# Score matmuls over 66 partitions, four convolution taps on TensorE, and three moved pieces of weight splitting in a two-block transformer kernel

## The chip, the cores and the metric

The kernel runs on one core of one Trainium2 chip. The metric is device time in microseconds; lower is better. The engines are named as in the profile: PE is TensorE, DVE is VectorE, ACT is ScalarE, POOL is GpSimd and SP is SyncE, which issues the loads.

## The reference

256 tokens of width 1024 pass through three layers. The first has an attention of 8 heads of 64 beside a causal depthwise convolution of 31 taps over 512 channels, then a gated feed-forward of width 2816. The second is a forgetting attention ("fox") of 16 heads of 64 with another such feed-forward; the third is a state-space mixer (S5) with a third feed-forward. Cut to what the change touches:

```python
q = apply_rope(rms_norm(q, q_norm_g[l]), cos, sin)      # first attention, per head of 64
k = apply_rope(rms_norm(k, k_norm_g[l]), cos, sin)
s_own = jnp.einsum('bhqd,bhkd->bhqk', qc, k_own).astype(jnp.float32) * scale
...
h = lax.conv_general_dilated(h, dw_w[:, None, :], ..., feature_group_count=CONV_WIDTH)   # 31 taps
x = x + jnp.concatenate([attn, conv], axis=-1) @ w_out[l]
x = x + (jax.nn.silu(h @ w_gate[l]) * (h @ w_up[l])) @ w_down[l]
...
log_f = jax.nn.log_sigmoid(f_logit + b_f)               # fox: one forget logit per head and token
c = jnp.cumsum(log_f, axis=1).transpose(0, 2, 1)
s = s + c[:, :, q0:k_end, None] - c[:, :, None, :k_end]
```

## The kernel before

All weights are read once, in units of 128 x 2048 float32 values (1 MB). SP loads a unit into one of four slots of `wraw`. ACT writes its high part (`split_high`, line 416) into a ring of two slots `whi`, and DVE the rest, the low part (`split_low`, line 422), into `wlo`. TensorE multiplies high and low parts of weights and of activations in three fp32r matmuls (lines 462 to 464, 482 to 484, 510) that add up in PSUM. Some units have other places for their parts (`early_gain`, `early_nat`, `early_qt`, with the low part over `wraw`). Each engine's order is written out by hand in `build`, and semaphores tie them together; an engine never passes an instruction that waits. A "quarter" (`mm_quarter`) is a quarter of a unit's contraction, six matmuls for both rows of 128 tokens.

*Ahead of the first attention* the units are q (0, 1), k (2, 3), u of the convolution (4 to 7) and v (8, 9). TensorE turns two heads at a time (`pe_heads`, line 1148) into two PSUM banks in alternation, and does one quarter of v after each such group; ACT copies the groups into `qt1` and `kt1` (`act_heads`, line 1188). ACT takes four sigmoids of u (`csig`, line 2020), and DVE multiplies them in (`glu`).

*In the first attention* each head has its scores (`scores`, lines 1055 and 1056: a 128x128 and a 128x256 matmul, each followed by a bf16 matmul that adds the mask), the maximum on DVE (line 1124), the exponential on ACT (line 1105), a turn on TensorE (line 1065) and the values (line 1074). Between them stand taps of the convolution: channel group 3 whole (31 taps, line 1631) and the last 10 taps of group 2 (line 1640) run on TensorE as matmuls with diagonal matrices that ACT makes (`tap_diagonals`, `shared_diagonals`); DVE does the other taps (line 2363). A float32 matmul is recorded as two.

*Into the feed-forward and into the fox units* (`add_and_turn` on DVE, `act_row_turn` on ACT, `mm_first_rows` on TensorE) the residual is added row by row of 128 tokens, turned on TensorE in tiles, and each turned tile is split into `actH` by ACT (line 630) and `actL` by DVE (line 637), while TensorE already multiplies the first two units with the tiles that are there.

*The forget gate* runs among the first fox units: `forget_logits` within the second unit, a copy `fT` on DVE, `forget_turned` on TensorE (two small transposes, line 1697), then on DVE and ACT the log of a sigmoid (lines 2509 to 2516, 2102, 2104), and its sums on TensorE (lines 1710 to 1712) ahead of the fifth fox unit. DVE's low part of the fourth fox unit stands within that arithmetic.

Of the kernel before, what the change touches and what calls it, by code (L numbers as in the profile page):

```python
# [17 lines left out]
F32 = mybir.dt.float32  # L18
# [3 lines left out]
ALU = mybir.AluOpType  # L22
AX = mybir.AxisListType

P = 128
TOK = 256
RT = TOK // P
D = 1024
KT = D // P
# [4 lines left out]
HD = 64  # L34
H1 = 8
H2 = 16
AW = H1 * HD
TAPS = 31
TAPG = 8
SHARED = 10  # L40
TAIL_PAIRS = {21: 19, 23: 20}
DIAGONALS_AT = {2: (0,), 3: (1, 2), 4: (3,), 5: (4,)}
U_BANKS = (2, 3, 6, 7)
ROWS_LOW, ROWS_HIGH = (0, 1, 2, 3), (4, 5, 6, 7)
# [9 lines left out]
UNIT = 2048  # L54
# [10 lines left out]
class Program:  # L65
# [121 lines left out]
    def place(self):  # L187
# [91 lines left out]
        self.csig = pen("csig", [P, 4, TOK])  # L279
        self.qn, self.kn = pen("qn", [P, RT, AW]), pen("kn", [P, RT, AW])  # L280
        self.vn = pen("vn", [P, RT, AW])
        self.qt, self.kt1 = pen("qt1", [HD, H1, TOK]), pen("kt1", [HD, H1, TOK])
        self.p1 = pen("p1", [P, 2, 384])
# [20 lines left out]
        pen = Pen(R0)  # L304
        AUG = HD + 2
        self.qa, self.ka = pen("qa", [P, RT, H2, AUG]), pen("ka", [P, RT, H2, AUG])
# [111 lines left out]
    def split_low(self, dve, n0, it=0):  # L418
# [4 lines left out]
                          self.high_of(n0).bitcast(F32), ALU.subtract).then_inc(self.lo_done, 1)  # L423

    def load_first(self, sp, view):

        for k in range(4):
            done = self.landed[0] if k == 3 else self.sem(f"first_landed{k}")
            sp.dma_start(self.wraw[:, 0, 512 * k:512 * k + 512], view[:, k, :]).then_inc(done, 16)
# [57 lines left out]

    def mm_first_rows(self, pe, st, n0, banks, order, between):


        for r, h in order:
            pe.wait_ge(self.lo_done, n0 + h + 1)
            for k in range(4):
                if (r, h, k) in between:
                    between[(r, h, k)]()
                pe.wait_ge(*self.past(st + "_act_ready", self.turn_count(st, r, 4 * h + k) + 1))
                self.mm_quarter(pe, n0 + h, banks, h, k, low=(self.lo_done, n0 + h + 1), rows=(r,))

# [419 lines left out]
    def pe_ffn(self, pe, st, turn, prep=False, last_units=1, half=None, end=None):  # L918
        n = self.first[st + ".up"]
        if st == "f1":  # L920
            self.mm_first_rows(pe, st, n, self.pair_banks(0), UNIT_BY_UNIT,
                               {(0, 0, 2): lambda: turn(1, 0), (0, 1, 2): lambda: turn(1, 1)})
# [289 lines left out]
def pool_constants(m, pool):  # L1212

    c = Chain(pool, m.sem("pool_chain"))
    for t, v in ((m.ident, 0.0), (m.ones, 1.0), (m.tri, 1.0), (m.swap, 0.0), (m.zerob, 0.0), (m.identb, 0.0), (m.maskb, 0.0),
                 (m.mhalf, -0.5), (m.halfpi, math.pi / 2), (m.hpad[:, :, 0:TAPS - 1], 0.0)):
        c.step(pool.memset(t[:] if not isinstance(t, bass.AP) else t, v))
# [224 lines left out]
def build(nc, io, out):  # L1442
    with ExitStack() as ctx:
# [145 lines left out]
        def _(pe):  # L1589
# [21 lines left out]
            m.pe_heads(pe, "a1", m.qn[:].rearrange("p r (h d) -> p r h d", d=HD), (0, H1), "q_ready", 2, (4, 5), 0,  # L1611
                       v_quarter)
            m.pe_heads(pe, "a1", m.kn[:].rearrange("p r (h d) -> p r h d", d=HD), (0, H1), "k_ready", 2, (4, 5),
                       H1 // 2, lambda f: v_quarter(4 + f))
# [3 lines left out]
            def conv(i):  # L1618

                if i == 3:  # L1620
                    pe.wait_ge(*m.past("v_out", 2))
                pair = i if i < 19 else TAIL_PAIRS.get(i)
                if pair is None:
# [70 lines left out]
            def forget_turned():  # L1694
                pe.wait_ge(*m.past("f_out", 1))
                for r in range(RT):
# [5 lines left out]
                            {(0, 0, 2): lambda: fp_turn(1, 0), (0, 1, 2): lambda: fp_turn(1, 1),  # L1702
                             (1, 1, 2): forget_logits})
            m.mm_half_k(pe, n + 2, (4, 5), 0)
            forget_turned()
            m.mm_half_k(pe, n + 3, (4, 5), 1)
# [242 lines left out]
        def _(act):  # L1949
# [67 lines left out]
            act.wait_ge(*m.past("k_head_sums", 1))  # L2017
            for j in range(4):
                act.wait_ge(m.used, first["u"] + 3 + j // 2)
                act.activation(m.csig[:, j, :], ps[:, U_BANKS[2 + j // 2], (j % 2) * TOK:(j % 2 + 1) * TOK],  # L2020
                               ACT.Sigmoid, bias=m.vec[:, GLUB + 4 + j:GLUB + 5 + j]).then_inc(sem("sig"), 1)
            act.activation(rinv[:, 0, 0:1], m.halfpi[:], ACT.Exp)
            m.act_heads(act, "a1", m.qt, (0, 4), (4, 5), 0)
            m.split_high(act, 9)
            m.act_heads(act, "a1", m.qt, (4, H1), (4, 5), 2)
            m.split_high(act, 10)
# [66 lines left out]
            m.act_row_turn(act, "fp", ROWS_HIGH, 1, range(4), MIXPRE)  # L2093
            for r in range(RT):
                m.act_row_turn(act, "fp", ROWS_HIGH, r, range(4, KT), MIXPRE)
            forget_high()
            m.split_high(act, first["fox"] + 2)
            for r in range(RT):
# [223 lines left out]
        def _(dve):  # L2322
# [55 lines left out]
            def head_norm1(st, banks, t, ki, rows):  # L2378
# [4 lines left out]
                for r in rows:  # L2383
                    rs = (m.rs, m.rsk)[ki][:, 8 * r:8 * r + 8].unsqueeze(2).to_broadcast([P, 8, HD])
                    c(dve.tensor_tensor(hd(m.rtmp[:]), hd(ps[:, banks[r], :]), rs, ALU.mult))
                    tb = [m.ropeg[:, ki, r, i:i + 1, :].to_broadcast([P, 8, HD]) for i in range(2)]
                    c.step(dve.tensor_tensor(hd(t[:, r, :]), hd(m.rtmp[:]), tb[0], ALU.mult))
                    halves = m.rtmp[:].rearrange("p (h a d) -> p h a d", a=2, d=32)
# [4 lines left out]
                    c.wait()  # L2393
                    dve.tensor_tensor(t[:, r, :], t[:, r, :], m.rtmp2[:], ALU.add).then_inc(sem(st + "_ready"), 1)
                    dve.wait_ge(*m.past(st + "_ready", r + 1))
# [16 lines left out]
            for j in range(2):  # L2412
                glu(j)
            conv(8)
            for j in range(2, 4):
# [67 lines left out]
            def add_and_turn(st, base, out, used, banks, gain, second_unit):  # L2483
# [3 lines left out]
                m.dve_row_turn(dve, st, banks, 1, range(4), gain)  # L2487
                m.split_low(dve, second_unit)
                m.dve_row_turn(dve, st, banks, 0, range(4, KT), gain)
                m.dve_row_turn(dve, st, banks, 1, range(4, KT), gain)  # L2490
# [11 lines left out]
            dve.wait_ge(*m.past("f_done", 1))  # L2502
            dve.tensor_copy(m.fT[:], ps[0:H2, 3, 0:TOK]).then_inc(sem("f_out"), 1)

            dve.wait_ge(*m.past("f_turned", 1))
            dve.wait_ge(*m.past("fb_in", 16))
            dve.wait_ge(*m.past("fp_rstd", RT))
            for r in range(RT):
# [4 lines left out]
               .then_inc(sem("f_abs"), 1)  # L2513
            m.split_low(dve, n + 3)
            dve.wait_ge(*m.past("f_ln", 1))
# [278 lines left out]
```

## Time and profile before

| | us |
|---|---|
| median of 3 runs (lowest, highest) | 989.36 (989.02, 989.72) |
| profiled execution | 988.04 |
| its span, first to last instruction | 986.2 |
| PE busy | 963.3 (98%) |
| DVE busy | 583.5 (59%) |
| ACT busy | 506.9 (51%) |
| POOL busy | 310.8 (32%) |

Times in the trace run from the start of the span. Busy times of matmuls overlap, since they are pipelined, so what a group of matmuls costs is read from start to start. A row of a timeline gives start, duration, engine, source line, operation, output and inputs, shape and count; the brackets give the idle time of the engine ahead of it and what ended it.

### The profile page before, as it was taken

The page shows a single profiled execution, that of the slowest core. Times are in us where ns is not written, and L with a number is a line of the kernel's source. Part 1 is how long each engine was busy: PE and PEld are TensorE (multiplying, and loading weights), DVE is VectorE, ACT ScalarE, POOL GpSimd, SP SyncE. Part 2 cuts the span into 40 slices and gives each one's busy share as a digit, 9 for nine tenths or more (in the row PEclk, how much of TensorE's full clock was granted, in tenths as well). Part 3 has the DMA queues.
Part 4 walks back from the last instruction along what each step waited for, and adds up shares of the span by engine and source line. Part 5 has one row for each costly group of instructions (what it writes and reads, how often), then busy time and mean ns, then how long its engine had stood idle before and what let it go on. Part 6 is the DMA issues. An engine that isn't in the chain of part 4 may idle for free.

```text
span 986.2 us, 14283 instructions
## 1 busy us (share of the span) xinstructions
PE 963.3 (98%) x5446; PEld 800.2 (81%) x5446; DVE 583.5 (59%) x639; ACT 506.9 (51%) x723; POOL 310.8 (32%) x331
## 2 busy tenths in 40 slices
PE   8999999999999989999999999999989999999997
PEld 6977777888888868888888888888978888888886
DVE  4898875554554456565774545546586755545544
ACT  6855465444443467456654444434456564444332
POOL 5670447999699216763010000000000020000000
PEclk9999999999999999999999999999999999999999
DMA  9842026676776746545446657557946456557551
GB/s 335 271 136 86 1 90 220 224 224 222 264 230 225 223 147 212 162 164 171 129 147 199 187 173 241 185 206 247 381 167 215 128 173 197 185 172 254 172 170 43
DMA packets 133827, 186.79 MB, mean 189 GB/s; under 512 B 5904, under 2 KB 104720, under 8 KB 133264
## 3 DMA queue, kind: packets, MB, share of 16 engines
q1 hardware_dynamic: 109632, 158.28, 49.3%
q10 hardware_dynamic: 24144, 27.81, 8.2%
q8 instruction: 35, 0.57, 0.3%
q14 instruction: 16, 0.13, 0.0%
HBM read 174.54 MB, written 15.73 MB: 193 GB/s over the span
## 4 chain that ended last, share of the span: by engine, by line
PE 91%; DVE 5%; ACT 2%; issue 1%; POOL 0%; DVEq 0%; POOLq 0%; ACTq 0%
PE ps L510 25%; PE ps L482 16%; PE ps L484 16%; PE ps L483 16%; PE ps L1055 2%; PE ps L462 2%; PE ps L464 2%; PE ps L463 2%; PE ps L839 1%; PE ps L1631 1%; PE ps L1074 1%; DVE wlo L422 1%; PE ps L1065 1%; PE ps L621 1%; PE ps L1160 1%
## 5 line engine op out<-in xcount | busy, mean ns | idle before, releaser
L422 DVE TENSOR_TENSOR wlo<-wraw,whi 128x2048 fp32r<-128x2048 f32 x127 | 302.0, 2380 | 293.1 <-ACT whi L416 293.1
L416 ACT ACTIVATE whi<-wraw 128x2048 fp32r<-128x2048 f32 x127 | 243.2, 1915 | 255.4 <-PE ps L484 156.3
L482 PE MATMUL ps<-whi,actH 128*128 128x512 f32 x640 | 258.0, 403 | 6.8 <-DVE wlo L422 5.9
L484 PE MATMUL ps<-whi,actL 128*128 128x512 f32 x640 | 250.2, 391 | 0.0
L483 PE MATMUL ps<-wlo,actH 128*128 128x512 f32 x640 | 249.4, 390 | 0.0
L482 PEld LDWEIGHTS ps<-whi,actH 128*128 128x128 f32 x640 | 120.3, 188 | 33.7 <-DVE wlo L422 6.5
L484 PEld LDWEIGHTS ps<-whi,actL 128*128 128x128 f32 x640 | 120.1, 188 | 26.1
L756 POOL TENSOR_SCALAR ss<-ss 128x1 f32<-128x1 f32 x8 | 1.8, 221 | 436.1 <-ACT sg L726 436.1
L483 PEld LDWEIGHTS ps<-wlo,actH 128*128 128x128 f32 x640 | 120.5, 188 | 22.3
L510 PE MATMUL ps<-whi,gH 128*128 128x512 f32 x248 | 77.8, 393 | 0.0
L510 PE MATMUL ps<-wlo,gH 128*128 128x512 f32 x248 | 76.8, 390 | 0.0
L510 PE MATMUL ps<-whi,gL 128*128 128x512 f32 x248 | 76.8, 389 | 0.0
L510 PEld LDWEIGHTS ps<-whi,gL 128*128 128x128 f32 x248 | 46.6, 188 | 9.8
L510 PEld LDWEIGHTS ps<-wlo,gH 128*128 128x128 f32 x248 | 46.6, 188 | 9.8
L510 PEld LDWEIGHTS ps<-whi,gH 128*128 128x128 f32 x248 | 45.9, 188 | 10.2 <-issue 1.2
L462 PE MATMUL ps<-actH,whi 128*128 128x256 f32 x160 | 45.6, 285 | 0.2 <-DVE wlo L422 0.2
L463 PE MATMUL ps<-actL,whi 128*128 128x256 f32 x160 | 45.3, 283 | 0.0
L464 PE MATMUL ps<-actH,wlo 128*128 128x256 f32 x160 | 45.3, 283 | 0.0
L877 ACT ACTIVATE gH<-ps 128x512 f32 (+1 forms) x33 | 19.8, 599 | 42.0 <-PE ps L839 42.0
L1105 ACT ACTIVATE p<-ps,nmax 128x128 f32<-128x128 f32 (+1 forms) x48 | 19.7, 417 | 34.6 <-DVE nmax L1124 34.6
L2363 DVE SCALAR_TENSOR_TENSOR cacc<-hpad,vectors,cacc 128x256 f32<-128x256 f32 x80 | 36.0, 521 | 0.0
L983 POOL TENSOR_TENSOR otmp<-G,Bri 128x512 f32 (+1 forms) x16 | 31.3, 1958 | 0.0
(452 smaller groups left out, 1573.7 us busy)
## 6 DMA issues: line engine op xcount, KB each, us to landing
wraw<-in_ffn_w_gate SPq DMA_DIRECT2D x44, 512.0 KB, 4.0
wraw<-in_ffn_w_up SPq DMA_DIRECT2D x44, 512.0 KB, 4.9
wraw<-in_ffn_w_down SPq DMA_DIRECT2D x18, 1024.0 KB, 4.9
wraw<-in_fox_w_in SPq DMA_DIRECT2D x16, 1024.0 KB, 5.4
wraw<-in_w_gate SPq DMA_DIRECT2D x22, 512.0 KB, 4.1
wraw<-in_w_up SPq DMA_DIRECT2D x22, 512.0 KB, 5.0
wraw<-in_w_in SPq DMA_DIRECT2D x9, 1024.0 KB, 11.2
wraw<-in_w_down SPq DMA_DIRECT2D x9, 1024.0 KB, 5.0
```

The lines of the kernel that those rows point to most:

```text
L416: act.activation(self.high_of(n0), self.wraw[:, n0 % RAW, :], ACT.Copy).then_inc(self.hi_done, 1)
L422: dve.tensor_tensor(self.low_of(n0), self.wraw[:, n0 % RAW, :], self.high_of(n0).bitcast(F32), ALU.subtract).then_inc(self.lo_done, 1)
L462: pe.matmul(out, wh, self.actH[:, k, :], start=(i == 0), stop=False)
L463: pe.matmul(out, wh, self.actL[:, k, :], start=False, stop=False)
L464: last = pe.matmul(out, wl, self.actH[:, k, :], start=False, stop=(i == KT - 1))
L482: pe.matmul(out, xh, wh, start=(ka == 0), stop=False)
L483: pe.matmul(out, xh, wl, start=False, stop=False)
L484: last = pe.matmul(out, xl, wh, start=False, stop=(ka == KT - 1))
L510: last = pe.matmul(self.ps[:, base + 2 * r + c, :], x, w[c], start=st, stop=sp_)
L877: act.activation(self.g_tiles(self.gH, f, f_step), self.ps[:, self.turn_bank(f0, at_end), :].rearrange("p (a b) -> p a b", a=2), ACT.Copy)\
L983: return pool.tensor_tensor(out, f[:, g, :].unsqueeze(3).to_broadcast([P, GB, n, SC]), w[:, g, :].unsqueeze(2).to_broadcast([P, GB, n, SC] ...
L2363: i = dve.scalar_tensor_tensor(m.cacc[:, j, :], src, w, m.cacc[:, j, :], ALU.mult, ALU.add)
```

## The change

1. `qn` and `kn` get two more columns a head, filled with zeros by POOL at the start, so that turned heads and scores have 66 partitions in place of 64.
2. `SHARED` goes from 10 to 14: four more taps of group 2 on TensorE, four fewer on DVE, whose taps are dealt out anew over the heads; the slots on TensorE and the diagonals on ACT follow.
3. Unit 9's high part goes between the sigmoids on ACT, its low part ahead of the last two `glu` on DVE.
4. In the first feed-forward and the fox units, the second unit's low part is made in two halves with two turned tiles between them, and the third unit's high part goes among ACT's turned tiles.
5. `forget_turned` goes into the third fox unit, and the fourth unit's low part ahead of the forget gate's arithmetic on DVE.

```diff
-SHARED = 10
-TAIL_PAIRS = {21: 19, 23: 20}
-DIAGONALS_AT = {2: (0,), 3: (1, 2), 4: (3,), 5: (4,)}
+SHARED = 14
+TAIL_PAIRS = {23: 22}
+DIAGONALS_AT = {3: (0, 1), 4: (2, 3), 5: (4, 5), 6: (6,)}
+AUG = HD + 2
...
-        self.qn, self.kn = pen("qn", [P, RT, AW]), pen("kn", [P, RT, AW])
+        self.qn, self.kn = pen("qn", [P, RT, H1, AUG]), pen("kn", [P, RT, H1, AUG])
...
-        self.qt, self.kt1 = pen("qt1", [HD, H1, TOK]), pen("kt1", [HD, H1, TOK])
+        self.qt, self.kt1 = pen("qt1", [AUG, H1, TOK]), pen("kt1", [AUG, H1, TOK])
...
+    def low_half(self, dve, n, i):
+
+        cols = slice(i * UNIT // 2, (i + 1) * UNIT // 2)
+        dve.wait_ge(self.hi_done, n + 1)
+        dve.tensor_tensor(self.low_of(n)[:, cols], self.wraw[:, n % RAW, cols],
+                          self.high_of(n)[:, cols].bitcast(F32), ALU.subtract)\
+           .then_inc(self.lo_done if i == 1 else self.sem("half_low"), 1)
...
         for r, h in order:
-            pe.wait_ge(self.lo_done, n0 + h + 1)
             for k in range(4):
...
-                self.mm_quarter(pe, n0 + h, banks, h, k, low=(self.lo_done, n0 + h + 1), rows=(r,))
+                first_half = half_low is not None and (r, h) == (0, 1) and k < 2
+                low = self.past("half_low", half_low) if first_half else (self.lo_done, n0 + h + 1)
+                self.mm_quarter(pe, n0 + h, banks, h, k, low=low, rows=(r,))
...
-                 (m.mhalf, -0.5), (m.halfpi, math.pi / 2), (m.hpad[:, :, 0:TAPS - 1], 0.0)):
+                 (m.mhalf, -0.5), (m.halfpi, math.pi / 2), (m.hpad[:, :, 0:TAPS - 1], 0.0),
+                 (m.qn[:, :, :, HD:AUG], 0.0), (m.kn[:, :, :, HD:AUG], 0.0)):
...
-                pair = i if i < 19 else TAIL_PAIRS.get(i)
+                pair = i if i < 22 else TAIL_PAIRS.get(i)
...
-            m.mm_half_k(pe, n + 2, (4, 5), 0)
-            forget_turned()
+            for k in range(4):
+                m.mm_quarter(pe, n + 2, (4, 5), 0, k)
+                if k == 1:
+                    forget_turned()
...
             for j in range(4):
+                if j == 2:
+                    m.split_high(act, 9)
                 act.wait_ge(m.used, first["u"] + 3 + j // 2)
...
-            m.act_heads(act, "a1", m.qt, (0, 4), (4, 5), 0)
-            m.split_high(act, 9)
-            m.act_heads(act, "a1", m.qt, (4, H1), (4, 5), 2)
+            m.act_heads(act, "a1", m.qt, (0, H1), (4, 5), 0)
...
-            for r in range(RT):
-                m.act_row_turn(act, "f1", ROWS_LOW, r, range(4, KT), N2)
+            m.act_row_turn(act, "f1", ROWS_LOW, 0, (4, 5), N2)
             m.split_high(act, 16)
+            m.act_row_turn(act, "f1", ROWS_LOW, 0, (6, 7), N2)
+            m.act_row_turn(act, "f1", ROWS_LOW, 1, range(4, KT), N2)
...
-            conv(4)
-            m.split_low(dve, 9)
-            conv(6)
+            conv(11)
             m.split_low(dve, 10)
...
-                    conv((6, 10, 11, 11, 11, 11, 2, 3)[h])
+                    conv((7, 8, 6, 9, 9, 9, 8, 4)[h])
```

Left out here: the low part of unit 9 goes behind `conv(8)` on DVE, and the fox units get on ACT what the last ACT piece gives unit 16. On DVE, around the fox units, the order was this (`wrawlow` is the second unit's low part, the first `wlo` the third unit's, the second the fourth's, `fl` the forget gate):

```order
L637 SCALAR_TENSOR_TENSOR actL<-ps,vectors,actH 128x128 x4
L422 TENSOR_TENSOR wrawlow<-wraw,early_nat 128x2048
L637 SCALAR_TENSOR_TENSOR actL<-ps,vectors,actH 128x128 x8
L2500 TENSOR_TENSOR wfL<-wf,wfH 128x128
L422 TENSOR_TENSOR wlo<-wraw,whi 128x2048
L2503 COPY fT<-ps 16x256
L2509 SCALAR_TENSOR_TENSOR fl<-ps,rx,fb 128x16 x2
L2512 SCALAR_TENSOR_TENSOR fl<-fl 128x32
L422 TENSOR_TENSOR wlo<-wraw,whi 128x2048
L2516 SCALAR_TENSOR_TENSOR fl<-fl 128x32
```

With the change it is this on the same engine, at the same place:

```order
L646 SCALAR_TENSOR_TENSOR actL<-ps,vectors,actH 128x128 x4
L429 TENSOR_TENSOR wrawlow<-wraw,early_nat 128x1024
L646 SCALAR_TENSOR_TENSOR actL<-ps,vectors,actH 128x128 x2
L429 TENSOR_TENSOR wrawlow<-wraw,early_nat 128x1024
L646 SCALAR_TENSOR_TENSOR actL<-ps,vectors,actH 128x128 x6
L2516 TENSOR_TENSOR wfL<-wf,wfH 128x128
L422 TENSOR_TENSOR wlo<-wraw,whi 128x2048
L2519 COPY fT<-ps 16x256
L422 TENSOR_TENSOR wlo<-wraw,whi 128x2048
L2526 SCALAR_TENSOR_TENSOR fl<-ps,rx,fb 128x16 x2
L2529 SCALAR_TENSOR_TENSOR fl<-fl 128x32
L2532 SCALAR_TENSOR_TENSOR fl<-fl 128x32
```

The second unit's low part is split around two tiles, and the fourth unit's low part has moved ahead of the three `fl` steps, the first of which waits for TensorE's turn.

On ACT, ahead of the first attention, the order was this (`csig` are the sigmoids, the first `whi` here is unit 9's high part, the second unit 10's):

```order
L2020 ACT_TABLE_LOAD
L2020 ACTIVATE csig<-ps,vectors 128x256 x4
L2022 ACT_TABLE_LOAD
L2022 ACTIVATE rinv<-halfpi 128x1
L1188 ACTIVATE qt_128<-ps 64x512 x2
L416 ACTIVATE whi<-wraw 128x2048
L1188 ACTIVATE qt_128<-ps 64x512 x2
L416 ACTIVATE whi<-wraw 128x2048
L1188 ACTIVATE kt_129<-ps 64x512 x4
```

With the change:

```order
L2034 ACT_TABLE_LOAD
L2034 ACTIVATE csig<-ps,vectors 128x256 x2
L416 ACTIVATE whi<-wraw 128x2048
L2034 ACTIVATE csig<-ps,vectors 128x256 x2
L2036 ACT_TABLE_LOAD
L2036 ACTIVATE rinv<-halfpi 128x1
L1197 ACTIVATE qt_128<-ps 66x512 x4
L416 ACTIVATE whi<-wraw 128x2048
L1197 ACTIVATE kt_129<-ps 66x512 x4
```

Unit 9's high part has moved ahead of two sigmoids and of all copies of queries.

## Rows read from the trace of the kernel before

**Rows 1.** The list of cores: span and mean granted clock.
```profile
core 0: 986.2 us, clock 0.999
```

**Rows 2.** The page's chain that ended last, shares of the span by engine.
```profile
PE 91%; DVE 5%; ACT 2%; issue 1%; POOL 0%; DVEq 0%; POOLq 0%; ACTq 0%
```

**Rows 3.** PE's waits, the two longest: us in total, times, longest us.
```profile
PE ps L482 <- DVE wlo L422: 5.9, 3, 2.9
PE ps L569 <- POOL zero L1234: 3.9, 1, 3.9
```

**Rows 4.** Timeline of PE ahead of the first attention: third and fifth head group, unit 9.
```profile
60.78 0.60 PE L1148 MATMUL ps<-ident,qn 128*64 128x128 f32 x4
...
64.44 0.60 PE L1148 MATMUL ps<-ident,kn 128*64 128x128 f32 x4
67.24 0.50 PE L482 MATMUL ps<-whi,actH 128*128 128x512 f32 x1 [2.21 <-DVE wlo L422]
```

**Rows 5.** Timeline of DVE there: first taps and unit 9's low part.
```profile
57.44 3.56 DVE L2363 SCALAR_TENSOR_TENSOR cacc<-hpad,vectors,cacc 128x256 f32<-128x256 f32 x6
...
64.36 2.83 DVE L422 TENSOR_TENSOR wlo<-wraw,whi 128x2048 fp32r<-128x2048 f32 x1
```

**Rows 6.** Timeline of ACT there: the last two sigmoids, the first two query copies.
```profile
57.33 0.84 ACT L2020 ACTIVATE csig<-ps,vectors 128x256 f32<-128x256 f32 x2 [1.63 <-PE ps L464]
...
59.59 1.06 ACT L1188 ACTIVATE qt<-ps 64x512 f32<-64x512 f32 x2
```

**Rows 7.** Timeline of PE in the first attention, one head: taps, scores, taps, turn, next scores.
```profile
86.70 1.08 PE L1631 MATMUL ps<-hpad,dtaps 128*128 128x256 f32 x4
87.71 0.48 PE L1055 MATMUL ps<-kt,qt 64*128 64x128 f32 x2
...
88.98 1.08 PE L1631 MATMUL ps<-hpad,dtaps 128*128 128x256 f32 x4
89.90 0.49 PE L1065 MATMUL ps<-ident,p 128*128 128x128 f32 x3
...
92.72 0.49 PE L1055 MATMUL ps<-kt,qt 64*128 64x128 f32 x2
```

**Rows 8.** Timeline of PE in the second attention: first score matmul, what follows the scores.
```profile
389.43 0.39 PE L1055 MATMUL ps<-kt,qt 66*128 66x128 f32 x2
...
390.23 0.48 PE L482 MATMUL ps<-whi,actH 128*128 128x512 f32 x1
```

**Rows 9.** Timeline of DVE in the first attention: the taps of one head.
```profile
91.94 4.44 DVE L2363 SCALAR_TENSOR_TENSOR cacc<-hpad,vectors,cacc 128x256 f32<-128x256 f32 x11
```

**Rows 10.** Timelines of PE and DVE, first feed-forward: second and third unit, second unit's low part.
```profile
146.43 0.47 PE L482 MATMUL ps<-early_nat,actH 128*128 128x512 f32 x1 [0.47 <-DVE actL L637]
154.19 0.50 PE L482 MATMUL ps<-whi,actH 128*128 128x512 f32 x1 [0.77 <-DVE wlo L422]
143.64 2.43 DVE L422 TENSOR_TENSOR wrawlow<-wraw,early_nat 128x2048 fp32r<-128x2048 f32 x1
```

**Rows 11.** Timelines of PE, ACT and DVE in the fox units: second, fourth and fifth unit.
```profile
351.17 0.47 PE L482 MATMUL ps<-early_nat,actH 128*128 128x512 f32 x1 [0.34 <-DVE actL L637]
365.56 0.29 PE L1697 MATMUL ps<-ident,fT 16*128 16x16 f32 x2
368.75 0.50 PE L482 MATMUL ps<-whi,actH 128*128 128x512 f32 x1 [2.90 <-DVE wlo L422]
374.90 0.48 PE L482 MATMUL ps<-whi,actH 128*128 128x512 f32 x1
358.93 1.90 ACT L416 ACTIVATE whi<-wraw 128x2048 fp32r<-128x2048 f32 x1
372.33 2.29 DVE L422 TENSOR_TENSOR wlo<-wraw,whi 128x2048 fp32r<-128x2048 f32 x1 [0.58 <-ACT whi L416]
```

**Rows 12.** Timeline of POOL at the start: the fill of hpad.
```profile
1.87 0.20 POOL L1217 MEMSET hpad<- 128x120 f32 x1
```

More of the change, by code:

```diff
@@ L304, in place @@
         pen = Pen(R0)
-        AUG = HD + 2
         self.qa, self.ka = pen("qa", [P, RT, H2, AUG]), pen("ka", [P, RT, H2, AUG])
@@ L486, in mm_quarter, with mm_first_rows @@
             last.then_inc(self.used, 1)
-    def mm_first_rows(self, pe, st, n0, banks, order, between):
+    def mm_first_rows(self, pe, st, n0, banks, order, between, half_low=None):
         for r, h in order:
-            pe.wait_ge(self.lo_done, n0 + h + 1)
             for k in range(4):
@@ L921, in pe_ffn @@
             self.mm_first_rows(pe, st, n, self.pair_banks(0), UNIT_BY_UNIT,
-                               {(0, 0, 2): lambda: turn(1, 0), (0, 1, 2): lambda: turn(1, 1)})
+                               {(0, 0, 2): lambda: turn(1, 0), (0, 1, 2): lambda: turn(1, 1)}, 1)
         else:
@@ L1610, in _ @@
             pe.wait_ge(*m.past("k_ready", 2))
-            m.pe_heads(pe, "a1", m.qn[:].rearrange("p r (h d) -> p r h d", d=HD), (0, H1), "q_ready", 2, (4, 5), 0,
+            m.pe_heads(pe, "a1", m.qn, (0, H1), "q_ready", 2, (4, 5), 0,
                        v_quarter)
-            m.pe_heads(pe, "a1", m.kn[:].rearrange("p r (h d) -> p r h d", d=HD), (0, H1), "k_ready", 2, (4, 5),
+            m.pe_heads(pe, "a1", m.kn, (0, H1), "k_ready", 2, (4, 5),
                        H1 // 2, lambda f: v_quarter(4 + f))
@@ L1702, in _ @@
                             {(0, 0, 2): lambda: fp_turn(1, 0), (0, 1, 2): lambda: fp_turn(1, 1),
-                             (1, 1, 2): forget_logits})
-            m.mm_half_k(pe, n + 2, (4, 5), 0)
-            forget_turned()
+                             (1, 1, 2): forget_logits}, 2)
+            for k in range(4):
+                m.mm_quarter(pe, n + 2, (4, 5), 0, k)
+                if k == 1:
+                    forget_turned()
             m.mm_half_k(pe, n + 3, (4, 5), 1)
@@ L2093, in _ @@
             m.act_row_turn(act, "fp", ROWS_HIGH, 1, range(4), MIXPRE)
-            for r in range(RT):
-                m.act_row_turn(act, "fp", ROWS_HIGH, r, range(4, KT), MIXPRE)
+            m.act_row_turn(act, "fp", ROWS_HIGH, 0, (4, 5), MIXPRE)
+            m.split_high(act, first["fox"] + 2)
+            m.act_row_turn(act, "fp", ROWS_HIGH, 0, (6, 7), MIXPRE)
+            m.act_row_turn(act, "fp", ROWS_HIGH, 1, range(4, KT), MIXPRE)
             forget_high()
-            m.split_high(act, first["fox"] + 2)
             for r in range(RT):
@@ L2386, in head_norm1 @@
                     tb = [m.ropeg[:, ki, r, i:i + 1, :].to_broadcast([P, 8, HD]) for i in range(2)]
-                    c.step(dve.tensor_tensor(hd(t[:, r, :]), hd(m.rtmp[:]), tb[0], ALU.mult))
+                    heads = t[:, r, :, 0:HD]
+                    c.step(dve.tensor_tensor(heads, hd(m.rtmp[:]), tb[0], ALU.mult))
                     halves = m.rtmp[:].rearrange("p (h a d) -> p h a d", a=2, d=32)
@@ L2393, in head_norm1 @@
                     c.wait()
-                    dve.tensor_tensor(t[:, r, :], t[:, r, :], m.rtmp2[:], ALU.add).then_inc(sem(st + "_ready"), 1)
+                    dve.tensor_tensor(heads, heads, hd(m.rtmp2[:]), ALU.add).then_inc(sem(st + "_ready"), 1)
                     dve.wait_ge(*m.past(st + "_ready", r + 1))
@@ L2414, in _ @@
             conv(8)
+            m.split_low(dve, 9)
             for j in range(2, 4):
                 glu(j)
-            conv(4)
-            m.split_low(dve, 9)
-            conv(6)
+            conv(11)
             m.split_low(dve, 10)
@@ L2487, in add_and_turn @@
                 m.dve_row_turn(dve, st, banks, 1, range(4), gain)
-                m.split_low(dve, second_unit)
-                m.dve_row_turn(dve, st, banks, 0, range(4, KT), gain)
+                m.low_half(dve, second_unit, 0)
+                m.dve_row_turn(dve, st, banks, 0, (4, 5), gain)
+                m.low_half(dve, second_unit, 1)
+                m.dve_row_turn(dve, st, banks, 0, (6, 7), gain)
                 m.dve_row_turn(dve, st, banks, 1, range(4, KT), gain)
@@ L2503, in _ @@
             dve.tensor_copy(m.fT[:], ps[0:H2, 3, 0:TOK]).then_inc(sem("f_out"), 1)
+            m.split_low(dve, n + 3)
             dve.wait_ge(*m.past("f_turned", 1))
@@ L2513, in _ @@
                .then_inc(sem("f_abs"), 1)
-            m.split_low(dve, n + 3)
             dve.wait_ge(*m.past("f_ln", 1))
```

## The prediction

> **What bounds the kernel now.** I read the list of cores first: the span is 986.2 us at a granted clock of 0.999, so TensorE stays at its upper level and no idle stretch in the span has lowered it [rows 1]. The chain of work that ended last is next: PE (TensorE) holds 91% of it, DVE (VectorE) 5%, ACT (ScalarE) 2% [rows 2]. So a change counts if it shortens TensorE's own work or one of the few stretches in which TensorE waits. The list of TensorE's waits gives the largest of those: the low part of a weight unit that DVE has not finished, 5.9 us in three places, and the start, where TensorE waits 3.9 us for GpSimd's constants [rows 3]. The rest is timelines of the places that the change edits. The sum is made against the profiled execution (988.04 us), which lies 1.32 us below the median of the runs shown (989.36); I apply the sum to the median.
>
> **1. Unit 9 earlier, before the first attention.** TensorE turns the heads of q and k in eight groups and does one quarter of the value units behind each. The fifth group starts at 64.44, and the quarter behind it, the first one of unit 9, only at 67.24, after 2.21 us of idle time that DVE's low part ends [rows 4]. That low part ran from 64.36 to 67.19, behind taps of the convolution [rows 5]. In the change the high part of unit 9 stands on ACT ahead of the third and fourth sigmoid, and the low part on DVE behind the first eight taps. Those sigmoids started at 57.33, when TensorE had finished the last u unit [rows 6]; the high part's ring slot comes free with the same unit, so it starts at 57.33 too and takes 1.90 (the same 128x2048 copy in [rows 11]). DVE's first taps end at 57.44 + 3.56 = 61.0, the low part (2.83) at 63.8, before TensorE wants it: the 2.21 us go. Late next are the query copies: behind the moved copy the first of them slips on ACT from 59.59 to 61.45 [rows 6]; half of the 1.06 for a pair later, at 62.0, its bank is free. TensorE's third group, at 60.78 [rows 4], needs that bank and now waits 1.2. After that the copies run in a row and find TensorE busy. So 2.2 − 1.2 = **1.0 us gained**; bounds 2.2 (no new wait) and 0.
>
> **2. Scores over 66 rows, four taps moved.** In the first attention the score matmuls of a head contract over 64 partitions: from the first (87.71) to the tap that follows (88.98) they take 1.27 us [rows 7]. In the second attention, where heads already have 66 partitions, the same four matmuls, of the same 128 and 256 columns, take 0.80 us (389.43 to 390.23) [rows 8]. That is 0.47 a head, 3.8 for eight. Two taps ahead of the scores take 1.01 (86.70 to 87.71), two behind them 0.92 (88.98 to 89.90) [rows 7]; if the 0.09 is the way into the other form, it goes too: 4.5. I take 4.2. Four more taps on TensorE at 0.46 each (half of 0.92) cost 1.8. Net **2.4 us gained**, bounds 2.0 and 2.7, as long as TensorE sets the pace. DVE does as much: eleven taps took 4.44 us, 0.40 each [rows 9], and the two reductions fill the rest of a head's 5.01 (87.71 to 92.72 [rows 7]), 0.6. With the change DVE has nine taps a head at most, 4.2 us, and TensorE 5.01 − 0.5 = 4.5. Both shrink, which either edit alone would not give: fewer rows' time on TensorE alone leaves DVE at 5.0. The diagonals of the extra taps go onto ACT, two pairs a head, where ACT waits for the reductions; I cost them at nothing, and if that cover is gone the tap behind them waits.
>
> **3. Halves in the first feed-forward.** TensorE idles 0.47 us before the second unit of the first pair (146.43) and 0.77 us before the third unit (154.19) [rows 10]. The first wait: DVE did the whole low part (2.43 us from 143.64 [rows 10]) and then the turned tiles that TensorE wanted. In the change it does half of it ahead of them, so they come 1.2 earlier, and 0.47 is less than that. The other half is due only two quarters and a turn of tiles later. The second wait: the third unit's high part stood on ACT behind all turned tiles and now stands ahead of the last six, so that DVE can take its low part as soon as its own turns end. Gain 0.47 + 0.77 = **1.2 us**; bounds 0.5 (only the first) and 1.3.
>
> **4. The fox units.** The same halves remove the 0.34 us at 351.17. The large wait is the 2.90 us at 368.75, for the low part of the fourth fox unit [rows 11]. Its high part was done at 360.8 (358.93 + 1.90), but on DVE the low part stood behind the forget gate's arithmetic, which needs a turn that TensorE did at 365.56, after the whole third unit. In the change the low part stands ahead of that arithmetic, and the turn comes after two quarters of the third unit. The low part can end at 360.8 + 2.3 = 363.1, TensorE asks for it at 365.85: the wait goes. The turn itself only changes place. Late next is the fifth unit: its low part ran from 372.33 to 374.62 and TensorE took it at 374.90, 0.28 later [rows 11]. TensorE comes 3.2 earlier; ACT's way to that unit (exponential, logarithm, key block, squares, high part) begins with the turn, which comes about 3 earlier as well. So 0.1 may remain: **3.1 us gained**, bounds 1.5 (the way to unit five moves by half) and 3.3.
>
> **5. Start.** GpSimd has two more small fills ahead of the constants on which TensorE starts; the fill of hpad, with more elements, took 0.20 [rows 12]. I take 0.2 for both, bounds 0 and 0.4. The copies of heads and the writes of qn and kn have as many columns as before: nothing.
>
> **Sum:** −1.0 − 2.4 − 1.2 − 3.1 + 0.2 = −7.5 us; 989.36 − 7.5 = **981.9 us** (980.5 against the profiled execution). Behind these places TensorE has no other wait of this size [rows 3], and the loads are released by its units and DVE's low parts, so what is gained is kept.
>
> [...] By rows 7 and 8, 64 rows cost 0.47 us a head more than 66. [...]
>
> **Rivals.**
> *66 rows gain nothing.* If the 0.47 belongs to the neighbours (taps in one attention, weight units in the other) and not to the 64 rows, part 2 is only its cost: −7.5 + 4.2 = −3.3, 986.1 us. For it: the neighbours do differ. Against it: between 87.71 and 88.98 there is no neighbour, and the whole difference is there. [...] Chance 0.06.
> *The time comes back at the next unit.* In part 4 the fifth unit and in part 1 the query copies are late next. If parts 4 and 1 gain only their lower bounds (1.5 and 0), the sum is −4.9: 984.5 us. For it: the slack at the fifth unit is 0.28. Against it: the work ahead of it starts with the turn that is moved. Chance 0.12.
> *Slower: the clock.* The new wait of 1.2 us near 60.8 lies just ahead of the first attention. If the granted clock fell there to its lower level (half) and stayed so through the heads, their 8 x 4.5 = 36 us on TensorE would take up to 36 more. From 7.5 us of work at the lower level on, the kernel is slower than before; with 12 it is at 993.9. Against it: waits of 2.21 and 2.90 us are in this span, whose clock is 0.999. Chance 0.02.
>
> **How the numbers follow.** A measurement of this kernel can tell 0.2%, 2 us, from no change. My forecast has 0.78, the two weaker gains 0.12 and 0.06, the clock 0.02; 0.02 is left for the two weaker gains at once, which lands near 989. Faster by over 2 us: 0.96, less 0.01 for the first rival with a weak part 3: 0.95. Slower 0.02, same 0.03. All upper bounds at once (2.2, 2.7, 1.3, 3.3, no cost) would be −9.5, 979.9 us, the low end. The high end takes in the second rival and reaches 985.2 for one more part at its lower bound.
>
> **What would show it.** Right: no idle time of TensorE before the fourth fox unit and the third feed-forward unit; some 1.2 us of it before the third head group and none before unit 9; score groups of 0.80 us; heads of some 4.5 us. Wrong: score groups still of 1.27; over 1 us of wait at the fifth fox unit; TensorE waiting for diagonals of taps or for DVE's reductions in the attention; a granted clock below 0.99.

## The result, and the profile after

| | before | with the change |
|---|---|---|
| median of 5 runs (lowest, highest) | 989.36 (989.02, 991.63) | 979.54 (979.15, 980.41) |
| profiled execution / its span | 988.04 / 986.2 | 980.41 / 978.5 |

The ratio is 0.9898, 95% interval 0.9884 to 0.9913: 9.8 us faster. The forecast was 7.5 us and 981.9; the measured time lies 0.36 below the low end, 979.9. But the two profiled executions differ by 7.63 only. So a reader who has just the two traces sees almost exactly the forecast, and 2.2 us of the gain are in neither. Where they are is the main question of what follows.

First the chain that ended last and TensorE's two longest waits, after (us in total, times, longest us):

```profile
PE 94%; DVE 3%; ACT 2%; issue 1%; POOL 0%; DVEq 0%; POOLq 0%; ACTq 0%
```
```profile
PE ps L578 <- POOL zero L1244: 4.1, 1, 4.1
PE ps L1157 <- ACT qt L1197: 1.1, 1, 1.1
```

PE's share of the chain went from 91 to 94%. The 5.9 us of waits for a low part in [rows 3] are gone; the second line is the new wait that the prediction expected at the third head group. PE in the v stage, in one head, and around the forget turn (start, duration, engine, line, operation, output and inputs, shape; idle time ahead in brackets):

```profile
62.87 0.63 PE L1157 MATMUL ps<-ident,qn 128*66 128x128 f32 x4 [1.12 <-ACT qt L1197]
...
85.58 0.38 PE L1064 MATMUL ps<-kt,qt 66*128 66x128 f32 x2
85.81 0.22 PE L1065 MATMUL ps<-maskb,identb 128*128 128x128 bf16 x1
85.86 0.65 PE L1064 MATMUL ps<-kt,qt 66*128 66x256 f32 x2
86.35 0.22 PE L1065 MATMUL ps<-maskb,identb 128*128 128x128 bf16 x1
86.41 1.08 PE L1641 MATMUL ps<-hpad,dtaps 128*128 128x256 f32 x4
...
90.06 0.38 PE L1064 MATMUL ps<-kt,qt 66*128 66x128 f32 x2
...
142.86 0.39 PE L490 MATMUL ps<-early_nat,actH 128*128 128x512 f32 x1
...
149.96 0.50 PE L490 MATMUL ps<-whi,actH 128*128 128x512 f32 x1
...
358.03 0.29 PE L1707 MATMUL ps<-ident,fT 16*128 16x16 f32 x2
...
361.11 0.39 PE L490 MATMUL ps<-whi,actH 128*128 128x512 f32 x1
...
367.15 0.50 PE L490 MATMUL ps<-whi,actH 128*128 128x512 f32 x1
```

The score group takes 0.83 us (85.58 to 86.41) where [rows 7] have 1.27, and a head 4.48 in place of 5.01. No bracket stands before the second and third unit of the feed-forward (142.86, 149.96), where [rows 10] have 0.47 and 0.77, nor before the fourth fox unit (361.11), where [rows 11] have 2.90, nor before the fifth (367.15), which the prediction named as late next.

The timeline of PE, cut at five landmarks, gives a table by stage for every trace of this study: *start* is the time of the first head group, *v* from there to the first score of the first attention, *a1* to the channel sums behind it, *o1* from the next turn to the second unit of the first feed-forward, *f1, fox* from there to the first score of the second attention. From that score to the end of TensorE's last matmul it takes 590.7 to 591.0 us in all traces; this is left out, as is the stretch between a1 and o1 (1.92 or 1.93, but in one run).

| trace | start | v | a1 | o1 | f1, fox |
|---|---|---|---|---|---|
| before, 988.04 | 57.12 | 17.23 | 37.54 | 32.62 | 243.00 |
| with the change, 980.41 | 57.92 | 15.91 | 35.10 | 32.00 | 238.85 |
| difference | +0.80 | −1.32 | −2.44 | −0.62 | −4.15 |

Behind the start that is 8.5 us; the start takes back 0.8, of which the fills explain 0.11 (first matmul at 4.06 in place of 3.95). The rest is TensorE's pace. TensorE's 24 turns of the input begin at 7.33 before and at 7.45 with the change; the rows are the same microsecond of both (length, busy time and number of these turns, clock, DMA share, GB/s), first before, then with the change:

```profile
9.00:10.00 1.00, 1.00 (x11) 1.00 1.02 393
9.00:10.00 1.00, 1.00 (x6) 1.00 1.06 403
```

Early turns start 0.21 us apart and later ones 0.11. The pace changes where the trace's own records of the granted clock begin, 8.56 us before and 10.06 with the change; ahead of the first record the column shows 1.00 all the same. So until then TensorE turns at half its later pace (0.21 against 0.11), and 1.50 us more of that are 0.75 of the 0.8. In the sixteen traces of this study the records begin between 5.07 and 10.06.

### The profile page after: what moved, and what is told of

It is laid out like the page before. It is cut to its first block, busy times and chain, and to the rows that moved or that the text cites. A ratio compares the mean times of both kernels' runs of the same rounds, so it can differ in the third digit from the quotient of the medians.

```text
span 978.5 us, 14303 instructions
## 1 busy us (share of the span) xinstructions
PE 961.0 (98%) x5454; PEld 803.0 (82%) x5454; DVE 581.8 (59%) x637; ACT 507.0 (52%) x727; POOL 309.9 (32%) x333
## 4 chain that ended last, share of the span: by engine, by line
PE 94%; DVE 3%; ACT 2%; issue 1%; POOL 0%; DVEq 0%; POOLq 0%; ACTq 0%
PE ps L519 25%; PE ps L490 17%; PE ps L492 16%; PE ps L491 16%; PE ps L470 2%; PE ps L1064 2%; PE ps L472 2%; PE ps L471 2%; PE ps L848 1%; PE ps L1641 1%; PE ps L1083 1%; PE ps L1074 1%; PE ps L630 1%; PE ps L1169 1%; PE ps L1020 1%
## 5 line engine op out<-in xcount | busy, mean ns | idle before, releaser
L1010 POOL TENSOR_TENSOR ob<-ob,otmp 128x576 f32<-128x576 f32 x16 | 34.6, 2160 | 1.3
```

The costliest lines, as they stand in the source:

```text
L1010: pool.tensor_tensor(o, o, t[:], ALU.add).then_inc(done, 1)
```

## The experiments

**The kernel before, three traces more.** The change's runs lie closer together than those of before, so the first question was whether the first trace of before is a typical one.

> The kernel before, unchanged, to get a second trace of it. Its first profiled span (986.2 us, 988.04 us in all) lies 1.3 us below the median of its runs, and the change's (978.5, 980.41) 0.9 us above the median of its own; so the two traces differ by 7.7 us and the medians by 9.8. Theory A: the difference lies in the start, where the 24 turns of the input took 3.56 us (7.33 to 10.89) before and 4.21 us (7.45 to 11.66) with the change, with the granted clock at 1.00 in both, and where the pace of the turns doubles near 8.7 before and near 10.0 with the change. Then this trace has a span of 987 to 988.5, the heads' turns begin at 58 or later instead of 57.12, and from there to the first score of the second attention it takes the same 332.3 us within 0.3. Rival B: the excess over 986.2 lies behind the start, in waits that the first trace lacks: start within 0.3 of 57.12, and over 1 us more behind it.

The median was 989.32. Its 11 runs and 40 more of before beside the other experiments lie in three clusters: 14 at 987.8 to 988.5, 27 at 988.9 to 989.9, 10 at 991.3 to 992.2. The first trace is of the lowest. This one, 991.71, is of the highest, and both theories fell short. The start was longer, 57.72, but v took 18.81 and f1, fox 244.6: 1.6 us more each, behind waits of the same length. The granted clock shows why. The rows are stretches of 2 us: length, PE busy (matmuls), clock, DMA share, GB/s:

```profile
368.00:370.00 2.00, 0.00 (x0) 1.00 0.79 295
370.00:372.00 2.00, 1.12 (x4) 0.91 0.97 227
372.00:374.00 2.00, 2.00 (x6) 0.50 1.00 394
374.00:376.00 2.00, 2.00 (x8) 0.73 1.01 382
```

TensorE idles 2.90 us for the low part of the fourth fox unit, and behind that the clock falls to 0.50: 6 matmuls in 2 us. Behind the 2.25 us for unit 9 it did the same, with 5 matmuls from 68 to 70 us. In the first trace the clock stayed up behind the same wait of 2.90, with 10 matmuls in 2 us:

```profile
368.00:370.00 2.00, 1.25 (x5) 1.00 0.93 231
370.00:372.00 2.00, 2.00 (x10) 1.00 1.01 396
```

Are the runs around the median between the two?

> The kernel before again, for a third trace. The runs of it so far lie in three clusters, near 988.0, near 989.3 and near 991.6 us; the trace at 988.04 has no fall of the granted clock, the one at 991.71 has two, behind the wait for unit 9 and behind the wait for the fourth fox unit. Theory: a run near 989.3 has one, behind the fourth fox unit, with 1.6 us more than the first trace from there to the first score of the second attention, and the rest of the difference in the start. Rival: the fall of such a run is in the v stage.

> The kernel before once more, for a fourth trace, with the same expectations as the run beside it: two falls of the granted clock near 991.6 us, one behind the fourth fox unit near 989.3, none near 988.0.

989.43 and 989.33: each has one fall, and not at the same place, so that theory and rival each held once. The first trace below (989.43) falls in the fox units, v is 17.23 and f1, fox 244.55; the second (989.33) falls in the v stage, 18.82 and 242.96.

```profile
368.00:370.00 2.00, 1.49 (x6) 1.00 0.99 289
370.00:372.00 2.00, 2.00 (x6) 0.50 1.00 367
372.00:374.00 2.00, 2.00 (x7) 0.65 0.93 336
```
```profile
66.00:68.00 2.00, 0.98 (x4) 1.00 0.00 0
68.00:70.00 2.00, 2.00 (x9) 0.58 0.83 287
70.00:72.00 2.00, 2.00 (x7) 0.56 0.58 238
```

So in these traces the clusters are none, one or two falls of the clock at 1.55 to 1.6 us, behind the two waits that the change removes. The runs without a trace agree in their mean granted clock: 0.999 or 1.000 in every run of the lowest cluster, 0.996 to 0.998 in the middle one, 0.993 to 0.996 in the highest. The start of these two was 56.95 and 56.87.

**The fox order back.**

```diff
             for k in range(4):
                 m.mm_quarter(pe, n + 2, (4, 5), 0, k)
-                if k == 1:
-                    forget_turned()
+            forget_turned()
...
-            m.split_low(dve, n + 3)
```
(on DVE the low part goes back in front of the last `fl` instruction)

> The change with the forget turn again behind the whole third fox unit, and the fourth unit's low part again within the forget gate's arithmetic; the halves are kept. My theory: TensorE waits 2.7 to 3.0 us again for the low part of the fourth fox unit, and none of it is taken back later: 982.2 to 982.7 us. Rival (the wait moves on to the fifth unit anyway): under 1.5 us more than with the change, under 981.0.

984.19, 4.65 more than the change, above the expectation: f1, fox took 243.42, 4.57 more. 2.90 is the wait, in the trace as it was; the rest is a fall of the clock to 0.50 behind it, and all five runs lie within 984.14 to 984.33.

**The same wait, filled.**

```diff
             forget_turned()
+            m.keep_warm(pe, 7, 12)
             m.mm_half_k(pe, n + 3, (4, 5), 1)
```

> The kernel with the forget gate's order of before (the run before it at 984.2), with 12 bf16 matmuls on 512 columns into a bank that nobody reads, put on TensorE ahead of the fourth fox unit, where it waits 2.9 us for the low part. Theory A (the fall of the granted clock behind that wait comes from TensorE's idling): the wait still costs its 3.0 us, but the clock stays at 1.00 behind it and the 1.6 us go: 982.4 to 982.9. Rival B (the fall has nothing to do with the idle time): 984.2 or more, with a stretch at 0.5.

983.17 (982.08 to 983.26): theory A by the trace. The wait keeps its price, f1, fox is 241.79, 2.94 more than with the change; the clock stays up and 1.63 us of the run before are gone. The median is 0.3 above the expectation; the runs spread by 1.2, and the three at 983.2 were not traced. Their mean granted clock, 0.999, is above the 0.998 of the traced run, whose clock falls only behind TensorE's last matmul (0.72 from 976 to 978 us, 0.50 from 978 to 980); so no fall shows in them either. First the run with the wait idle, then with it filled:

```profile
360.00:362.00 2.00, 0.26 (x3) 1.00 0.89 335
362.00:364.00 2.00, 0.85 (x2) 0.84 0.90 214
364.00:366.00 2.00, 2.00 (x6) 0.50 0.93 358
```
```profile
360.00:362.00 2.00, 2.00 (x11) 1.00 0.82 305
362.00:364.00 2.00, 1.80 (x9) 1.00 0.96 226
```

So it is TensorE's idling that lets the clock fall there: to 0.50 behind 2.90 us of it, and not with the 0.20 us of it that the filling leaves.

**Unit 9 back.**

```diff
-                if j == 2:
-                    m.split_high(act, 9)
...
+            m.act_heads(act, "a1", m.qt, (0, 4), (4, 5), 0)
+            m.split_high(act, 9)
+            m.act_heads(act, "a1", m.qt, (4, H1), (4, 5), 2)
```
(and the low part again behind `conv(4)`, which follows the last `glu`)

> The change with unit 9's two parts where they were (high part between the query copies, low part behind the second taps). TensorE should wait 2.2 us for that low part again and lose the 1.1 us wait at the third head group: +1.1 us on the way from the heads' turns to the first score. Theory A (a wait of over 2 us lets the granted clock fall to 0.5 behind it in part of the executions, at 1.6 us a fall): the runs lie in two clusters, near 980.6 and near 982.2, with a fall in the v stage in those of the upper one. Rival B (the fall comes from something else, or only where two waits of this size are in the span): all runs near 980.6.

980.53 (980.26 to 981.34): rival B. The wait is there again (2.23 at 67.79), v is 17.15, 1.24 more than with the change, but the mean clocks of the five runs are 0.999 to 1.000, where runs of before with one fall have 0.996 to 0.998. A wait of this length was followed by a fall in two of four traces of before (2.25 and 2.24 us; not behind 2.21 in the two others); in these five runs none shows. What decides it is open.

**64 rows.**

```diff
+ROWS1 = HD
...
-        self.qn, self.kn = pen("qn", [P, RT, H1, AUG]), pen("kn", [P, RT, H1, AUG])
+        self.qn, self.kn = pen("qn", [P, RT, H1, ROWS1]), pen("kn", [P, RT, H1, ROWS1])
```
(the same for `qt` and `kt1`, and without the two fills)

> The change with 64 rows in place of 66 in the first attention, all else kept (fourteen shared taps too). My theory: 64 rows cost 0.47 us a head, so a score group goes from 0.83 back to 1.27 to 1.30 us, and from the first score to the channel sums it takes 35.1 + 3.5 to 4.0 = 38.6 to 39.1 us; the time is 983.0 to 983.6. Rival (the neighbours, not the rows, set the score group): 0.83 a group and 35.1 us, 979.5 in all.

983.74; a1 took 39.31, 0.53 a head more than with 66 rows. Both lie just above what was expected, by 0.1 and 0.2. PE, one head:

```profile
86.42 0.48 PE L1065 MATMUL ps<-kt,qt 64*128 64x128 f32 x2
86.84 0.23 PE L1066 MATMUL ps<-maskb,identb 128*128 128x128 bf16 x1
87.00 0.70 PE L1065 MATMUL ps<-kt,qt 64*128 64x256 f32 x2
87.63 0.23 PE L1066 MATMUL ps<-maskb,identb 128*128 128x128 bf16 x1
87.69 1.08 PE L1641 MATMUL ps<-hpad,dtaps 128*128 128x256 f32 x4
```

From a score to its mask matmul it takes 0.42 and 0.63 here, 0.23 and 0.49 with 66 rows; from the first mask to the next score 0.16 and 0.05. The taps ahead of the first score take 1.01 in place of 0.92. The loss stands at each passage between 64 and 128 rows. To tell it from a slower matmul, the passages were halved:

```diff
+            for i, mask in enumerate((self.maskb, self.zerob, self.maskb)):
+                pe.matmul(self.ps[:, b, i * P:(i + 1) * P], self.identb[:], mask[:], start=(i == 0), stop=False)
             for r in range(RT):
...
-                out = self.ps[:, b, c0:c0 + nk]
-                pe.matmul(out, qt[:, h, r * P:(r + 1) * P], kt[:, h, 0:nk], start=True, stop=False)
-                last = pe.matmul(self.ps[:, b, c0 + nk - P:c0 + nk], self.identb[:], self.maskb[:],
-                                 start=False, stop=True)
+                last = pe.matmul(self.ps[:, b, c0:c0 + nk], qt[:, h, r * P:(r + 1) * P], kt[:, h, 0:nk],
+                                 start=False, stop=(r == 1))
```

> The change with 64 rows, as in the run with 64 rows, but with a head's mask matmuls (and one of zeros, so that all columns are opened) put ahead of its two score matmuls instead of each behind one: TensorE goes from 128 rows to 64 and back once a head, not twice. Only the stretch of the first attention is read. Theory A (the passage between 64 and 128 rows costs): half of the 0.53 us a head goes, less 0.06 for the matmul of zeros: a head takes 4.75 to 4.85 us (5.01 with 64 rows, 4.47 with 66), the stretch from the first score to the channel sums 37.4 to 38.0 us. Rival B (a matmul of 64 rows is slower in itself, or its weight load): 5.0 us a head or more, 39.3 us or more.

```profile
86.04 0.22 PE L1063 MATMUL ps<-maskb,identb 128*128 128x128 bf16 x1
86.09 0.22 PE L1063 MATMUL ps<-zerob,identb 128*128 128x128 bf16 x1
86.15 0.22 PE L1063 MATMUL ps<-maskb,identb 128*128 128x128 bf16 x1
86.30 0.92 PE L1066 MATMUL ps<-kt,qt 64*128 64x128 f32 x4
87.14 1.13 PE L1641 MATMUL ps<-hpad,dtaps 128*128 128x256 f32 x4
...
90.84 0.22 PE L1063 MATMUL ps<-maskb,identb 128*128 128x128 bf16 x1
```

A head takes 4.80 us (86.04 to 90.84), a1 37.50: theory A. Less the 0.05 of the matmul of zeros, one way into 64 rows and back costs 0.27 a head (4.75 against 4.48), two cost 0.53, so nothing is left for the rows themselves. This run also passes between bf16 and float32 only once a head; that costs nothing visible, since with 66 rows a score follows its mask matmul after 0.05 (85.81 to 85.86), as here one mask matmul follows another (86.04 to 86.09).

**Ten shared taps.**

```diff
-SHARED = 14
+SHARED = 10
...
-                    conv((7, 8, 6, 9, 9, 9, 8, 4)[h])
+                    conv((6, 10, 10, 11, 11, 11, 2, 3)[h])
```
(`TAIL_PAIRS`, `DIAGONALS_AT` and the number of taps ahead of the tail as before)

> The change with 10 shared taps on TensorE and 83 on VectorE as before, 66 rows kept. My theory: VectorE then sets the pace, eleven taps and two reductions of a head need 5.0 us, so TensorE's 1.3 us shorter head buys little and the stretch from the first score to the channel sums takes 36.5 to 37.5 us in place of 35.1: 981 to 982 us. Rival (TensorE alone sets the pace): four taps of 0.45 less, 33.3 us, 977.7 us.

982.64, a1 37.02. VectorE sets the pace: TensorE waits 1.92 us for the last heads' exponentials, which follow VectorE's maxima. The clock falls behind this wait too:

```profile
104.86 0.55 PE L1074 MATMUL ps<-ident,p 128*128 128x128 f32 x3 [1.92 <-ACT p L1114]
```
```profile
108.00:110.00 2.00, 2.00 (x12) 0.50 0.00 0
110.00:112.00 2.00, 2.00 (x6) 0.50 0.00 0
112.00:114.00 2.00, 2.00 (x9) 0.62 0.00 0
```

At 0.50 the clock stays for 6.8 us here, and for 3.4 in each of the five other falls ahead of TensorE's last matmul. The same turn and value matmuls as with the change take 1.30 us more at the end of a1, and from a1 to o1 it takes 3.52 in place of 1.92; so it cost 2.9. Without it a1 would be 35.7, worked out from these rows: below the 36.5 to 37.5 that were expected, well above the rival's 33.3. So the mechanism held, and the stretch reached the expected size only by the fall; the time is 0.6 above the expectation. One of the five runs, 980.55 at a clock of 0.998 (the others 0.996), lies 2 us below the others.

**The halves back**, in both places:

```diff
-                m.low_half(dve, second_unit, 0)
-                m.dve_row_turn(dve, st, banks, 0, (4, 5), gain)
-                m.low_half(dve, second_unit, 1)
-                m.dve_row_turn(dve, st, banks, 0, (6, 7), gain)
+                m.split_low(dve, second_unit)
+                m.dve_row_turn(dve, st, banks, 0, range(4, KT), gain)
```
(and the third unit's high part on ACT behind all turned tiles)

> The change with the second unit's low part made at once again and the third unit's high part behind all turned tiles, in the first feed-forward and in the fox units. My theory: the waits 0.47, 0.77 and 0.34 us come back, 1.4 to 1.6 us, all too short for the clock: 980.9 to 981.2, granted clock as with the change. Rival (these waits are taken back at the next unit): under 0.7 us more, under 980.3.

981.42 (980.97 to 981.89), 1.9 more and 0.2 above the expectation: the waits come back and stay, no fall of the clock (0.999 in all five runs). By stage +0.57 in o1 and +1.23 in f1, fox, where the brackets of before were 0.47, and 0.77 + 0.34 (1.58 in all).

**Improvements.** Unit 9's high part behind the first query copy:

```diff
+            m.act_heads(act, "a1", m.qt, (0, 2), (4, 5), 0)
+            m.split_high(act, 9)
+            m.act_heads(act, "a1", m.qt, (2, H1), (4, 5), 1)
```

> The change with unit 9's high part behind the first query copy instead of ahead of two sigmoids, and its low part behind the last two products of sigmoids. My theory: the new 1.1 us wait at the third head group goes, and the low part is done as TensorE asks for it, so it waits under 0.4 us there: 978.4 to 978.9. Rival (the low part is late again): a wait of over 0.8 us before unit 9, no gain, 979.3 to 980.

978.33 (977.99 to 979.05), just below the expectation. v is 14.66: neither wait is left in the trace. Then, with the change's own order of unit 9, 12 shared taps (slots and diagonals follow):

```diff
-SHARED = 14
+SHARED = 12
...
-                    conv((7, 8, 6, 9, 9, 9, 8, 4)[h])
+                    conv((7, 8, 6, 9, 9, 9, 9, 5)[h])
```

> The change with 12 shared taps in place of 14, the two that return to VectorE in the last two heads, where it waits 0.29 and 0.69 us for TensorE. If TensorE alone sets the pace, 0.9 us less (two taps of 0.45): 34.2 us from the first score to the channel sums, 978.6. If VectorE takes over in these heads, nothing or worse: 35.1 us or more, and a wait of TensorE behind the last head.

978.64, a1 34.19: as expected. And the start, added to the kernel at 978.33 (the two fills go behind all constants):

```diff
+    c(pool.memset(m.identb[:], 0.0))
+    c.step(pool.affine_select(out=m.identb[:], ...))
...
-            pe.wait_ge(*m.past("consts", 1))
-            m.keep_warm(pe, 7, 8)
+            pe.wait_ge(sem("pool_chain"), 2)
+            m.keep_warm(pe, 7, 13)
+            pe.wait_ge(*m.past("consts", 1))
```

> The kernel with unit 9's high part between the query copies (978.3), and the start changed: GpSimd makes the bf16 identity first, TensorE's warming matmuls start on it (13 instead of 8), and the two fills of qn and kn stand behind all constants. Theory A (the spread of 1 to 1.4 us among runs of one kernel lies in the start, where TensorE's pace doubles at another moment in each): the first matmul starts near 1.5 instead of 4.06, the 24 turns run at the doubled pace from the beginning, the first weights' product starts at 10.3 to 10.6 in the trace, and the runs spread by under 0.5 us around 977.6 to 978.1. Rival B (the spread comes from the loads): the runs spread by 1 us as before and the median stays within 0.2 of 978.3.

978.12 (977.79 to 978.47). PE, its first three groups:

```profile
1.59 5.73 PE L578 MATMUL ps<-identb 128*128 128x512 bf16 x13 [1.59 <-POOL identb L1225]
7.11 3.07 PE L584 MATMUL ps<-rdiag,x_res 128*128 128x128 f32 x24
10.31 0.47 PE L490 MATMUL ps<-whi,actH 128*128 128x512 f32 x1
```

The trace is as theory A has it, the median nearer to rival B: 0.2 less, and a spread of 0.7, not under 0.5. Not settled, then, for the spread of the start: TensorE's pace still doubles at different moments, with the trace's first record of the clock, at 7.22 in this one and at 5.07 in that of the next run. All three together:

> The three improvements together: unit 9's high part between the query copies, the start with the identity first, 12 shared taps. They lie in different stretches, so they should add up: 978.12 (the first two) less 0.9 for the taps, 977.0 to 977.4. If VectorE is late in the last heads after the earlier start: 977.8 or more.

977.13 (977.04 to 977.22), ratio to before 0.988 (0.9859 to 0.9901): they add up, 2.4 us below the change.

## Why the prediction was wrong

**The step that failed** stands in its first part: "so TensorE stays at its upper level and no idle stretch in the span has lowered it", and "I apply the sum to the median". The first trace has no fall of the clock ahead of TensorE's last matmul, but the two traces of runs at the median of before have one each, worth 1.55 to 1.6 us, behind one of the two waits that parts 1 and 4 remove. The sum put this term at nothing. The 1.32 us between that trace and the median were named and not asked after. The clock was a rival, but as a loss for the new wait of 1.2 us (1.12 measured), where no trace shows a fall; the waits of 2.2 and 2.9 us were taken as harmless because one trace had let them pass.

**The account.** By the traces, the change saves 8.5 us behind the start, where parts 1 to 4 had 7.7: 0.8 of the miss is their size, and the larger piece is the fall. A median run of before takes a fall of 1.55 more. Together 10.1; the measured 9.8 leave 0.3, within what the starts differ (56.9 in the two traces of median runs of before; with the change 57.92 in its only trace, whose span is 0.9 above that of the median run; 56.7 to 57.6 in seven other traces with that start). No trace of a median run of the change exists, so this last piece is inferred.

In what follows the brackets hold what the prediction had, and the figure behind them is the measured one.

**Part 1** (1.0): 1.32. The mechanism was right, the wait for unit 9 gone and one of 1.12 at the third group (1.2 expected). A wait costs more than its bracket: from the fifth group to its quarter it took 2.80 us [rows 4], and 0.35 where nothing waits (57.92 to 58.27 with the change), so 2.45, not 2.21. In the prediction's working the slipped copy starts at 61.49 (59.59 and 1.90), not 61.45, which changes nothing.

**Part 2** (2.4): 2.44. A head gained 0.53, as the working with the way into the other form had it (4.2 for eight, measured 4.21 with the rows alone undone). That the two edits need each other was right in the runs as they are: a1 is 37.02 with the rows alone, 39.31 with the taps alone, 37.54 with neither and 35.10 with both. But "fewer rows' time on TensorE alone leaves DVE at 5.0" says too much: without the fall behind the wait, the rows alone come to 35.7, a gain of 1.8. The number of taps was not the best one: 12 give 34.19. The run with half the passages puts one way there and back at 0.27 us and leaves nothing for the rows themselves; what TensorE does in these 0.27 us, no run shows.

**Parts 3 and 4** (1.2 and 3.1): together 0.62 + 4.15 = 4.8 against 4.3; all four waits are gone, and the fifth unit is not late. Undone alone, the halves cost 1.8 in the trace, the fox order 2.9 without the clock.

**Part 5** (0.2): the two fills move the first matmul by 0.11. The rest of the trace's 0.8 is not the change: TensorE's pace doubled 1.50 us later in this execution, and the moment differs among traces of one kernel too (first record of the clock at 8.56, 9.84, 8.17 and 6.89 in the four of before).

**Rivals.** That 66 rows gain nothing is excluded by the run with 64. The time does not come back at the next unit, since no wait stands there. The clock did matter, but the other way round: its falls had lengthened the kernel before, by 1.55 to 1.6 us each.

## What to carry to other kernels

When the profiled execution and the median of the runs differ by more than the runs differ among themselves, that difference is a term of the sum: ask which stretch of the profile could hold it, and whether the change removes that stretch. A wait of TensorE can cost more than its length: here a fall of the clock to 0.50 behind waits of 2.24 to 2.90 us cost 1.55 to 1.63 us more; filling the one of 2.90 with matmuls that nobody reads kept the clock at 1.00, and removing it was worth both. Before splitting work between TensorE and VectorE, work out both paces: here fewer rows' time alone left TensorE waiting 1.92 us for VectorE's maxima and the exponentials behind them, and two of the four taps moved were two too many.

## What the runs showed of the hardware

- Behind waits of TensorE of 1.92, 2.24, 2.25 and 2.90 us the granted clock fell to 0.50, for 6.8 us behind the first and 3.4 behind each of the longer ones; behind other waits of 2.21, 2.23 and 2.90 us it stayed at 1.00, and behind waits of 1.13 us or less no trace shows a fall while TensorE still has work. One fall cost 1.55 to 1.63 us behind the longer waits, and 2.9 behind the 1.92.
- Filling the wait of 2.90 us with matmuls that nobody reads kept the clock at 1.00 in the trace of that run.
- Passing from 128 rows to 64 and back cost 0.27 us: 0.53 a head for two such passages, around 128 and around 256 columns, and 0.27 for one around both.
- In the start TensorE turned at half its later pace (0.21 us a turn against 0.11) until the trace's first record of the granted clock, which lay between 5.07 and 10.06 us; the rows of the view show 1.00 there too, because there is no record. The 24 turns took from 2.87 us, where the records begin at 7.50, to 4.09, where they begin at 10.06.
